# Late mixer weights: from full fp32 matmuls to high and low parts split inside the ring, one tile at a time

## The reference

```python
x = x + FFN_HALF * swiglu(rms_norm(x, ffn1_norm[l]), ffn1_w_gate_up[l], ffn1_w_down[l])
u = rms_norm(x, mix_norm[l]) @ w_in[l]            # 1024 -> 5144 columns
u_ssd, u_ml, u_rw = jnp.split(u, [D_SSD_IN, D_SSD_IN + D_MLSTM_IN], axis=-1)
y = jnp.concatenate([ssd_mixer(u_ssd, ...), mlstm_mixer(u_ml, ...), rwkv7_mixer(u_rw, ...)], axis=-1)
x = x + y @ w_out[l]
x = x + FFN_HALF * swiglu(rms_norm(x, ffn2_norm[l]), ffn2_w_gate_up[l], ffn2_w_down[l])
```

## Time and profile before

| what | value |
|---|---|
| three runs | 1769.57, 1773.21, 1773.78 us; median 1773.21 |
| profiled execution, time | 1773.07 us |
| its span (first to last instruction) | 1771.2 us |
| TensorE clock granted, mean | 0.978 of full |
| PE busy | 1697.9 us (96% of the span) |
| PEld busy | 1537.2 us (87%) |
| DVE busy | 1291.2 us (73%) |
| ACT busy | 932.7 us (53%) |
| POOL busy | 407.0 us (23%) |
| fp32 matmuls of the late tiles (L1066) | 191.7 us in 832 instructions |
| loads of 1 MB into the ring | 205, median 4.8 us from issue to landing |

### The profile page before, as it was taken

One profiled execution on the slowest core, in us unless ns is written; L12 is line 12 of the kernel. 1 busy time (PEld: TensorE's weight loads), 2 busy tenths in 40 slices (PEclk: granted clock), 3 DMA queues, 4 the chain that ended last, 5 costly groups with the idle time before them and its releaser, 6 DMA issues.

```text
span 1771.2 us, 32697 instructions
## 1 busy us (share of the span) xinstructions
PE 1697.9 (96%) x13812; PEld 1537.2 (87%) x13812; DVE 1291.2 (73%) x2141; ACT 932.7 (53%) x1666; POOL 407.0 (23%) x316
## 2 busy tenths in 40 slices
PE   7999999999799999999999999979999999989998
PEld 6888998888698888888899888879888898979987
DVE  5887775865667887688777586566787676789974
ACT  5774536323446764577443632344676455556652
POOL 2772000000213761177200000021376200021110
PEclk9999999999799999999999999979999999989999
DMA  6675622211046665666552221105565543335442
GB/s 254 239 278 186 220 102 96 93 53 43 32 167 250 235 235 172 222 245 224 195 216 95 96 96 49 50 26 178 216 247 202 199 172 120 120 143 191 173 150 105
DMA packets 45057, 282.67 MB, mean 160 GB/s; under 512 B 6128, under 2 KB 6768, under 8 KB 18544
## 3 DMA queue, kind: packets, MB, share of 16 engines
q1 hardware_dynamic: 44912, 280.60, 43.8%
HBM read 279.53 MB, written 1.05 MB: 158 GB/s over the span
## 4 chain that ended last, share of the span: by engine, by line
PE 85%; DVE 10%; ACT 3%; issue 1%; POOL 1%; DMA 1%; SPq 0%; DVEq 0%; ACTq 0%
PE banks L531 27%; PE banks L532 14%; PE banks L1066 8%; PE banks L523 7%; PE banks L524 7%; PE banks L525 7%; PE banks L1673 3%; DVE WL L494 2%; ACT WH L489 1%; PE banks L1942 1%; PE banks L570 1%; DVE ML L1440 1%; DMA ring<-wst 1%; PE banks L1952 0%; PE banks L738 0%
## 5 line engine op out<-in xcount | busy, mean ns | idle before, releaser
L494 DVE TENSOR_TENSOR WL<-ring,WH 128x2048 fp32r<-128x2048 f32 (+1 forms) x219 | 459.9, 2111 | 110.8 <-ACT WH L489 110.6
L531 PE MATMUL banks<-XNP,WH 128*128 128x512 f32 x1408 | 498.4, 399 | 10.9 <-DVE XNP L616 8.8
L489 ACT ACTIVATE WH<-ring 128x2048 fp32r<-128x2048 f32 (+1 forms) x223 | 380.8, 1716 | 53.5 <-PE banks L525 46.6
L532 PE MATMUL banks<-XNP,WL 128*128 128x256 f32 x1408 | 392.9, 279 | 0.0
L531 PEld LDWEIGHTS banks<-XNP,WH 128*128 128x128 f32 x1408 | 265.8, 189 | 73.2 <-DVE XNP L616 9.9
L964 POOL TENSOR_TENSOR HP<-G,HP 128x256 fp32r<-128x256 f32 x110 | 210.3, 1913 | 309.8 <-ACT HP L776 309.8
L531 PE MATMUL banks<-HP,WH 128*128 128x512 f32 x770 | 267.5, 392 | 0.8 <-POOL HP L964 0.7
L532 PEld LDWEIGHTS banks<-XNP,WL 128*128 128x128 f32 x1408 | 266.6, 189 | 0.0
L532 PE MATMUL banks<-HP,WL 128*128 128x256 f32 x770 | 215.2, 280 | 0.0
L1066 PE MATMUL banks<-XN,ring 128*128 128x256 f32 x832 | 191.7, 381 | 0.0
L531 PEld LDWEIGHTS banks<-HP,WH 128*128 128x128 f32 x770 | 144.5, 188 | 33.2 <-POOL HP L964 1.4
(11 more groups left out here) (496 smaller groups left out, 3285.6 us busy)
## 6 DMA issues: line engine op xcount, KB each, us to landing
ring<-wst SPq DMA_DIRECT2D x205, 1024.0 KB, 4.8
ring<-wst SPq DMA_DIRECT2D x80, 704.0 KB, 4.1
LP<-lp SPq DMA_DIRECT2D x1, 1872.0 KB, 7.4
LP<-lp SPq DMA_DIRECT2D x4, 448.0 KB, 5.5
ring<-wst SPq DMA_DIRECT2D x2, 512.0 KB, 5.5
X<-xin SPq DMA_DIRECT2D x2, 512.0 KB, 6.3
out<-X SPq DMA_DIRECT2D x4, 256.0 KB, 2.2
C<-cst SPq DMA_DIRECT2D x1, 193.0 KB, 5.0
```

The lines of the kernel that those rows point to most:

```text
L489: e.do.activation(WH[:, slot[q], 0:n], ring[:, i % NSLOT, 0:n], ACT.Copy).then_inc(*w_act.up("high", q))
L494: e.do.tensor_tensor(WL[:, slot[q], 0:n], ring[:, i % NSLOT, 0:n], WH[:, slot[q], 0:n].bitcast(F32), ALU.subtract).then_inc(*w_dve.up("low ...
L531: e.do.matmul(b[:, :], WH[:, s, cols], x.rearrange("p s t -> p (s t)"), start=first, stop=False)
L532: return e.do.matmul(b[:, 0:T], WL[:, s, cols], x[:, 0, :], start=False, stop=last)
```

## The change

The late 13 blocks of each layer are now split too, but in the ring itself. Each of their 26 tiles gets a slot of its own: SP loads 128 x 1024 floats (0.5 MB, gathered in runs of 128 floats = 512 B) into the first half of a slot; ACT writes the high part into the slot's second half, and DVE writes the low part over the landed floats. Both go in two halves of 512 columns. The normed x is split as well: its high parts go to eight places that are free at that time (three in `G2`, two in `LP`, one in `AL`, two in `GAP`), its low parts over `XN`. PE then runs three fp32r matmuls where it ran one in fp32. So three slots hold three tiles and no longer three blocks of two. The load of tile i waits for PE's end of tile i - 3. The distance table `AL` of the attention is loaded late, since its place holds a high part before.

```diff
+        holds, item = [], []
+        for i, (name, l, what) in enumerate(plan):
+            item.append(len(holds))
+            holds.extend((i, s) for s in range(2 if by_tiles(name, what) else 1))
...
+        def slot_at(i, s=0):
+            return (item[i] + s) % NSLOT
...
-            return f_pool.on("ada", ...) if name == "w_ada_2" else p_pe.on("tile", l, 2 * what[1] + 1)
+            return f_pool.on("ada", ...) if name == "w_ada_2" else p_pe.on("tile", l, 2 * what[1] + s)
...
+        xh_late = [G2r[:, i, 1, :] for i in range(3)] + [LPr[...] for i in range(2)] + [
+            ALr[:, 0:T]] + [GAPr[:, T * i:T * i + T] for i in range(2)]
+        def split_tile(i):
+            return {10: 14, 12: 15}.get(i) if i < 14 else i + 2 if i < 38 else None
+        def act_tile_high(e, l, i, half):
+            at = slice(512 * half, 512 * half + 512)
+            b = place["w_in", l, ("two", i // 2)]
+            e.wait_ge(*landed(b, i % 2))
+            e.do.activation(tile_parts(l, i, at)[1], ring[:, slot_at(b, i % 2), at], ACT.Copy).then_inc(*w_act.up("tile high", l, i, half))
+        def dve_tile_low(e, l, i, half):
+            ...
+            e.wait_ge(*w_act.on("tile high", l, i, half))
+            e.do.tensor_tensor(low, ring[...], high.bitcast(F32), ALU.subtract)...
+        def act_x_high(e, l, k):
+            e.wait_ge(*p_dve.on("normed", l, k // 4 * 4))
+            if k >= 6:
+                e.wait_ge(*p_pe.on("tile", l, 2 * EARLY - 1))
+            e.do.activation(xh_late[k], XN[:, k, :], ACT.Copy).then_inc(*p_act.up("xh", l, k))
+        def dve_x_low(e, l, k):
+            e.wait_ge(*p_act.on("xh", l, k))
+            e.wait_ge(*s_pe.on("gates", l))
+            e.do.tensor_tensor(XNr[:, k, :], XN[:, k, :], xh_late[k].bitcast(F32), ALU.subtract)...
...
         def pe_proj(e, l):
-                                wt = ring[:, place["w_in", l, ("two", n)] % NSLOT, :]
-                                m = e.do.matmul(b[:, 0:T], wt[:, at], XN[:, kt, :], start=kt == 0, stop=kt == KT - 1)
+                                if kt == 4 * half:
+                                    e.wait_ge(*w_dve.on("tile low", l, i, half))
+                                if i == 2 * EARLY:
+                                    e.wait_ge(*p_act.on("xh", l, kt))
+                                    e.wait_ge(*p_dve.on("xl", l, kt))
+                                wl, wh = tile_parts(l, i, slice(kt * 128, kt * 128 + 128))
+                                e.do.matmul(b[:, 0:T], wh, xh_late[kt], start=kt == 0, stop=False)
+                                e.do.matmul(b[:, 0:T], wh, XNr[:, kt, :], start=False, stop=False)
+                                m = e.do.matmul(b[:, 0:T], wl, xh_late[kt], start=False, stop=kt == KT - 1)
...
         def act_proj(e, l):
             for i in range(43):
-                yield
+                if split_tile(i):
+                    act_tile_high(e, l, split_tile(i), 0)
+                yield
+                if split_tile(i):
+                    act_tile_high(e, l, split_tile(i), 1)
...
         def dve_proj(e, l):
             for i in range(43):
+                if i and split_tile(i - 1):
+                    dve_tile_low(e, l, split_tile(i - 1), 1)
                 yield
...
+                if split_tile(i):
+                    dve_tile_low(e, l, split_tile(i), 0)
                 yield
...
         def sync(e):
+                if by_tiles(plan[i][0], plan[i][2]):
+                    both = wst[i].rearrange("p (k s t) -> p k s t", k=KT, s=2)
+                    for s in range(2):
+                        e.wait_ge(*freed(item[i] + s - NSLOT))
+                        e.do.dma_start(ring[:, slot_at(i, s), 0:1024].rearrange("p (k t) -> p k t", k=KT), both[:, :, s, :]).then_inc(
+                            s_slot[slot_at(i, s)], 16)
```

More of the change, by code:

```diff
@@ L72, in in_parts, with by_tiles @@
     return name != "w_ada_2" and not (name == "w_in" and what[1] >= EARLY)
+def by_tiles(name, what):
+    return name == "w_in" and what[1] >= EARLY
 def blocks():
@@ L475, in freed @@
                 return low_on(turn[i])
-            return f_pool.on("ada", what[1] // 6, what[1] % 6) if name == "w_ada_2" else p_pe.on("tile", l, 2 * what[1] + 1)
+            return f_pool.on("ada", what[1] // 6, what[1] % 6) if name == "w_ada_2" else p_pe.on("tile", l, 2 * what[1] + s)
         def in_turn(q, free):
@@ L488, in act_high @@
             e.wait_ge(*landed(i))
-            e.do.activation(WH[:, slot[q], 0:n], ring[:, i % NSLOT, 0:n], ACT.Copy).then_inc(*w_act.up("high", q))
+            e.do.activation(WH[:, slot[q], 0:n], ring[:, slot_at(i), 0:n], ACT.Copy).then_inc(*w_act.up("high", q))
         def low_part(e, q):
@@ L747, in ada_block @@
             at = place["w_ada_2", 0, ("two", 6 * f + n)]
[L748 removed]
+            return at, ring[:, slot_at(at), :]
         def act_ada(e, f, n):
@@ L1034, in split_at, with tile_parts @@
             return i % 2 == 1 and i // 2 < EARLY - AHEAD
+        xh_late = [G2r[:, i, 1, :] for i in range(3)] + [LPr[:, LC["wig"] + T * i:LC["wig"] + T * i + T] for i in range(2)] + [
+            ALr[:, 0:T]] + [GAPr[:, T * i:T * i + T] for i in range(2)]
+        def tile_parts(l, i, at):
+            slot = slot_at(place["w_in", l, ("two", i // 2)], i % 2)
+            return ringr[:, slot, at], ringr[:, slot, 1024 + at.start:1024 + at.stop]
+        def split_tile(i):
[6 more added lines that the diff above has]
+        def dve_tile_low(e, l, i, half):
+            at = slice(512 * half, 512 * half + 512)
+            low, high = tile_parts(l, i, at)
+            e.wait_ge(*w_act.on("tile high", l, i, half))
+            e.do.tensor_tensor(low, ring[:, slot_at(place["w_in", l, ("two", i // 2)], i % 2), at], high.bitcast(F32), ALU.subtract).then_inc(
+                *w_dve.up("tile low", l, i, half))
+        def act_x_high(e, l, k):
[6 more added lines that the diff above has]
+            e.wait_ge(*s_pe.on("gates", l))
+            e.do.tensor_tensor(XNr[:, k, :], XN[:, k, :], xh_late[k].bitcast(F32), ALU.subtract).then_inc(*p_dve.up("xl", l, k))
         def pe_proj(e, l):
@@ L1053, in pe_proj @@
                             e.wait_ge(*low_on(turn_of("w_in", l, ("two", n))))
-                        else:
-                            e.wait_ge(*landed(place["w_in", l, ("two", n)]))
-                            e.wait_ge(*p_dve.on("normed", l, 4))
                     if i < 40:
```

59 lines of the change are left out of this document (44 added, 15 removed).

## The result

The changed kernel takes 1800.1 us in the median (1799.6 to 1801.1), the kernel before 1773.2 beside it: a ratio of 1.0156, with a 95% interval of 1.0143 to 1.0169. The forecast of 1785 had the direction right and the size wrong: 12 us were expected and 27 came. The time lies inside the range of 1764 to 1806 only because that was wide.

The account below looks back on a forecast made before the run. PE was taken to bound the first and third stretch, DVE the second. A layer's +4 + 4.5 - 2.5 = +6 us, for two +12, on 1773.07 gave 1785 us, range 1764 to 1806.

Parts of the forecast that it names:

- PE's gain, 0.57 us a tile: On PE, 24 split matmuls take 2.88 us where 16 fp32 instructions took 3.45; 29.6 us over 52 tiles.
- C to D: First layer, from PE's matmul that waits for MS to the mLSTM's closing sums: about -4 us.
- Landing taken as 5 us: In the ring, the load time of a 0.5 MB tile in runs of 512 B; bounds 3.7 and 6.
- my argument from packets: Landing time from 1024 packets at 523 a us, 2.0 us, plus about 2.8 us: 4.8 us.
- First stretch, the rounds on ACT: First 64 us: high parts waiting for landings delay ACT's later work in each round; +4 us at 316.
- A: Start of the first RWKV matmul on PE in the first layer; put 2.2 us later.
- B: Start of the first matmul of the head sums on PE, first layer; put 5.7 us later.
- rival 1: The split pays, PE remains the bound and ring waits are covered: 1756 us; with a half-gain version, chance 0.23.
- The pieces of x, 0 (upper end 1 us a layer): Splitting x beside PE's tiles 7 to 13 comes about when tile 14 needs it, so costs nothing.
- Second stretch, +4.5: The 29 us where DVE is the chain: low parts 3.6 us plus ACT's landing waits; bounds 3 and 7.
- The clock, counted 0: PE's granted clock stays at 1.00 in all stretches as long as PE stays this busy; no gain or loss.
- Rival 3: The ring is the clock of the projection, from a landing of about 5.8 us: +30, 1803 us; chance 0.18.

Follow-up runs that it names:

- e14: The changed kernel with all 26 tiles split, but at tile 14 the eight products with x's low parts come last: 1794.7 us.
- e5: The changed kernel plus 16 unused fp32 filler matmuls a layer at three of PE's waits: 1786.9 us.
- e2: The changed kernel without DVE's 52 low parts a layer; PE multiplies the high part in their place: 1782.9 us.
- e3: The changed kernel with GpSimd making the high parts in place of ACT: 1791.5 us.
- e6: The changed kernel with weights stored so that a tile is read in runs of 4 KB, not 512 B: 1792.9 us.
- e4: The changed kernel with the high parts, and the low parts behind them, of tiles 16 to 39 one tile later in the order: 1822.9 us.
- after: The changed kernel itself, all 26 late tiles a layer split, against the kernel before: 1800.1 us.
- e8: The changed kernel with GpSimd making the second half of each tile's low parts, DVE the first: 1807.3 us.

## Why the prediction was right in sign and wrong in size

- **PE's gain, 0.57 us a tile: right where the clock holds.** Starts are 0.12 us apart, and there are 416 = 52 x 8 of each of the three matmuls. C to D gains 3.0 us, where the same reckoning gives about 4.
- **Landing taken as 5 us: too high**, 4.2 measured. The straight line's 3.8 was nearer than my argument from packets. In that argument the 2.8 us set beside the packets stands on no row: the ring's loads run at up to 437 GB/s in the trace of before, where 1 MB takes 2.4 us and leaves 2.5 of 4.9. By the Trainium skill's estimate (3.2 us; DMA: Bandwidth & Descriptors, Anatomy of one DMA, a fit made on transfers that GpSimd issues) the landing should have been shorter still; the run does not reach it even with runs of 4 KB (3.7). The rule in the Trainium skill (same page, Specifications) that runs of 512 B reach the full rate is not borne out here: they land 0.5 us later than runs of 4 KB. On its own this error would have made the forecast too high.
- **First stretch, the rounds on ACT: the step that failed.** The prediction said of the rounds behind A that "the next round is alike" and priced them: GG +5.2, RV +5.7, then catching up to +4 at 316. Measured are GG +10.5, RV +11.4 and B +13.1. A itself was put at +2.2 and came at +4.0. Of this 2.2 us come from tile 14 (next point): without its wait (e14) A is at +1.8. From A to B the prediction allows some 3.5 us and 9.1 came. The rounds were priced with PE at full clock and DVE free. Neither was so. Behind the wait at A, PE ran at 1.2 GHz to 285 us, and with fillers A to B is 3.5 us shorter (e5). DVE's low parts lie on the chain before B, and without them it is 1.9 us shorter (e2); I counted them only in the second stretch. With the landing waits off ACT it is 6.5 us shorter (e3). These overlap and are no sum. Nor did ACT catch up: that it has 46 us of work in 64 is a share, the very argument I held against rival 1.
- **The pieces of x, 0 (upper end 1 us a layer): wrong.** PE waits 1.82 us at tile 14 for a low part of x, and the clock falls to the lower level for the tiles behind it. e14 takes 5.4 us away, 2.7 a layer, though 1.27 us of wait remain.
- **Second stretch, +4.5: right in sum, perhaps by luck.** B to C is +4.4, where the prediction's steps make +4.5. Fillers (e5) cut it to +2.1 and long runs (e6) to +1.7 without a change on DVE, so it wasn't DVE's low parts alone.
- **The clock, counted 0: the other term that failed.** The first paragraph let it stay out "as long as PE stays this busy", but the sum makes PE stand 2.2 us longer at A alone, and puts no price on what follows. The clock did fall (0.87, 0.91 and 0.96), and e5 shows that it is worth at least 13.2 of the 27 us, nearly all of the 15 that the forecast missed. I had named it as what would put the time above my range.
- **Rival 3** (1803) had the time nearly right with another mechanism, so by luck: it needed a landing of 5.8 us (5.5 by its own sum of 10.9 us a round), and 4.2 were measured.

Summed: the forecast's two layers are +12; D is 14.5 us late in the first layer and 29.5 in the second, and the time is 27 more. Where the 2 to 3 us behind D come back, no run tells.

## What to carry to other kernels

When TensorE, always busy before, gets idle times of about two microseconds or more, price each twice: once as itself and once for the matmuls that run at 1.2 GHz behind it. Above all, put no wait for a transfer into an in-order engine ahead of other strands' work: shares of busy time don't tell that cost, and in a ring of three single tiles neither of the two places tried for it was good (e4, after). In this kernel the split paid only where the unit that it relieves is the chain: eight tiles of 26, with the products of late operands ordered last, gave -0.4%, and all 26 gave +1.6%.

## What the runs showed of the hardware

- In after, one idle time of 1.82 us on PE was followed by 1 us of matmuls at the old rate and then 3.4 us with starts 0.21 us apart (257.9 to 261.3); behind one of 3.76 us PE was slow until 285.2. Idle times of up to 0.81 us in the kernel before, and one of 1.27 us in e14, were followed by stretches with a granted clock of 1.00. 16 unused matmuls a layer made the kernel 13.2 us faster (e5).
- 512 KB in runs of 512 B land in 4.2 us (after), in runs of 4 KB in 3.7 (e6); 1 MB in 4.7 to 4.9.
- GpSimd's cast of 128x512 to fp32r takes 893 ns (ACT 629), its subtraction 1446 ns (DVE 684). GpSimd at work beside it slows DVE: its subtraction takes 746 ns in e3 and 725 in e8, and in e8 it is as busy with 310 instructions as in after with 341.
